# Expert weights in two loads with semaphores of their own, and ring places given back by kind

## The reference

```python
def moe_ffn(h, router_w, router_bias, w_gate, w_up, w_down, s_gate, s_up, s_down):
    top_idx, top_w = route(h, router_w, router_bias)          # 8 of 64 experts for each token
    ...
    yb = lax.map(lambda a: swiglu(a[0], w_gate[a[1]], w_up[a[1]], w_down[a[1]]), (xb, blk_exp))
    ...
    return swiglu(h, s_gate, s_up, s_down) + routed
```

## Time and profile before

| | us |
|---|---|
| median of 3 runs (3470.9 to 3479.81) | 3478.23 |
| the profiled execution | 3474.74 |
| its span | 3472.9 |
| PE busy in the span | 3048.3 (88%) |
| VectorE, ScalarE, POOL busy | 1299.7, 1015.3, 515.6 |

### The profile page before, as it was taken

One profiled execution on the slowest core, in us unless ns is written; L12 is line 12 of the kernel. 1 busy time (PEld: TensorE's weight loads), 2 busy tenths in 40 slices (PEclk: granted clock), 3 DMA queues, 4 the chain that ended last, 5 costly groups with the idle time before them and its releaser, 6 DMA issues. The chain is left out here.

```text
span 3472.9 us, 64620 instructions
## 1 busy us (share of the span) xinstructions
PE 3048.3 (88%) x24428; PEld 1627.9 (47%) x24429; DVE 1299.7 (37%) x2708; ACT 1015.3 (29%) x1799; POOL 515.6 (15%) x534
## 2 busy tenths in 40 slices
PE   6998989979989999999978998899898778867796
PEld 3554668955533333333324546689553223322231
DVE  3434633445433333333354435344443222212234
ACT  2223542222222332333343324422222212222232
POOL 0100005231011111111051100052311000000004
PEclk8998999999999999999989999999899889978898
DMA  9202320032369998998874103200335889887866
GB/s 382 101 10 101 131 88 3 4 132 85 146 230 353 357 354 316 377 358 352 350 285 163 48 7 146 64 3 4 144 158 230 326 338 362 346 338 308 347 262 230
DMA packets 133673, 724.22 MB, mean 209 GB/s; under 512 B 24800, under 2 KB 42720, under 8 KB 96736
## 3 DMA queue, kind: packets, MB, share of 16 engines
q1 hardware_dynamic: 84800, 544.14, 40.4%
q0 software_dynamic: 28224, 102.77, 7.8%
q10 hardware_dynamic: 20448, 74.46, 5.2%
HBM read 619.62 MB, written 101.71 MB: 208 GB/s over the span
## 5 line engine op out<-in xcount | busy, mean ns | idle before, releaser
L2287 PE MATMUL psum<-arena 128*64 x1792 | 830.3, 618 | 184.9 <-DVE arena L2389 184.9
L2289 PE MATMUL psum<-arena 128*64 128x512 f32 x1792 | 830.3, 618 | 0.0
L2287 PEld LDWEIGHTS psum<-arena 128*64 128x64 f32 x1792 | 245.0, 142 | 680.5 <-issue 680.5
L827 PE MATMUL psum<-arena 128*128 128x480 f32 (+3 forms) x1088 | 405.4, 530 | 15.8 <-PEq L164 8.3
L2309 PE MATMUL psum<-arena 128*64 x896 | 408.3, 599 | 12.1 <-DVE arena L2392 8.8
L2311 PE MATMUL psum<-arena 128*64 128x512 f32 x896 | 408.5, 599 | 0.0
L2257 POOL DMA_INDIRECT arena<-h,arena x112 | 141.8, 1266 | 1367.9 <-PE psum L2277 1344.6
L827 PEld LDWEIGHTS psum<-arena 128*128 128x128 f32 x1088 | 209.1, 195 | 190.6 <-issue 178.2
L2356 ACT COPY arena<-arena 128x2048 f32 x114 | 215.9, 1894 | 249.8 <-DMA arena<-in_w_dn 238.8
L2309 PEld LDWEIGHTS psum<-arena 128*64 128x64 f32 x896 | 120.0, 138 | 280.2 <-issue 280.1
L2289 PEld LDWEIGHTS psum<-arena 128*64 128x64 f32 x1792 | 245.0, 142 | 0.0
(11 more groups left out here) (359 smaller groups left out, 4328.7 us busy)
## 6 DMA issues: line engine op xcount, KB each, us to landing
arena<-in_w_gu SPq DMA_DIRECT2D x130, 2048.0 KB
arena<-in_w_dn SPq DMA_DIRECT2D x130, 1024.0 KB
y_slots<-arena ACTq DMA_DIRECT2D x122, 512.0 KB, 10.4
arena<-in_ada SPq DMA_DIRECT2D x24, 2048.0 KB, 7.8
y_slots<-arena SPq DMA_DIRECT2D x4, 4096.0 KB
arena<-in_w_gdn SPq DMA_DIRECT2D x6, 1536.0 KB
arena<-in_w_out SPq DMA_DIRECT2D x2, 4096.0 KB
arena<-in_w_tok SPq DMA_DIRECT2D x4, 1920.0 KB
```

The costliest lines, as they stand in the source:

```text
L827: last = nc.tensor.matmul(bank(n, wide), lhsT[:, k], rhs[:, k], start=(k == 0), stop=(k == DK - 1))
L2287: nc.tensor.matmul(psum[half(0), 2 + r, :], xT[:, r, rows_of(k, 0)], W[:, bass.ds(at + k * 2 * DE, 2 * DE)], start=(k == 0), stop=(k == DK ...
L2289: last = nc.tensor.matmul(psum[half(1), 2 + r, :], xT[:, r, rows_of(k, 1)], late_gu[:, k * 2 * DE:(k + 1) * 2 * DE], start=(k == 0), stop= ...
```

## The change

`w_in` is replaced by two pairs of semaphores, `g_in` for gate/up loads and `d_in` for down loads. The copies of gate/up wait on `g_in` alone, and `copy_dn` gets a wait on `d_in`. A ring place's gate/up part is loaded again when `gu_done` (not `units_done`) has reached the former expert's last unit; the down part still waits on `units_done`. The wait for the load two before is by kind too. The loader still issues gate/up and then down of each expert, in order. The plan holds one row with the late expert's number in place of two rows with semaphore counts; the engines work the counts out of it. The plan values are read one unit at a time, right before `gate`, `copy_dn` and `product`, and no longer at the top of the loop.

```diff
+                        def load_gu(e):
+                            if e >= WRING:
+                                free[e] = sp.value_load(plan[0:1, T_FREE + e - WRING:T_FREE + e - WRING + 1], min_val=1, max_val=NU)
+                                sp.wait_ge(gu_done, free[e])
+                            sp.wait_ge(g_in[e % 2], 16 * (e // 2))
+                            at = e % WRING * WSLOT
+                            sp.dma_start(W[:, at:at + GU], A["w_gu"][...]).then_inc(g_in[e % 2], 16)
+
+                        def load_dn(e):
+                            if e >= WRING:
+                                sp.wait_ge(units_done, free[e])
+                            sp.wait_ge(d_in[e % 2], 16 * (e // 2))
+                            at = e % WRING * WSLOT + GU
+                            sp.dma_start(W[:, at:at + DN], A["w_dn"][...]).then_inc(d_in[e % 2], 16)
+
                         for e in range(3, NE):
-                            r = e % WRING
-                            if e >= WRING:
-                                free = sp.value_load(plan[...], min_val=1, max_val=NU)
-                                sp.wait_ge(units_done, free)
-                            sp.wait_ge(w_in[e % 2], 32 * (e // 2))
-                            sp.dma_start(... A["w_gu"] ...).then_inc(w_in[e % 2], 16)
-                            sp.dma_start(... A["w_dn"] ...).then_inc(w_in[e % 2], 16)
+                            load_gu(e)
+                            load_dn(e)
...
+                def wait_weights(eng, sems, e):
+
+                    eng.wait_ge(sems[0], ((e >> 1) << 4) + 16)
+                    eng.wait_ge(sems[1], ((e + 1) >> 1) << 4)
...
                     @block.vector
                     def _(dve):
-                        def copy_gu(need, at):
-                            for r in range(2):
-                                dve.wait_ge(w_in[r], need[r])
+                        def copy_gu(e, at):
+                            wait_weights(dve, g_in, e)
                             nc.vector.tensor_copy(late_gu[:, 0:GU // 2], W[:, bass.ds(at, GU // 2)]).then_inc(lg_ready, 1)
 
-                        def copy_dn(at):
+                        def copy_dn(e, at):
+                            wait_weights(dve, d_in, e)
                             nc.vector.tensor_copy(late_dn[:, :], W[:, bass.ds(at + GU, DN)]).then_inc(ldn_ready, 1)
...
                         later = later_pairs(dve)
-                        early = [slot(dve, u, 1) for u in range(3)]
-                        need = [weights(dve, u) for u in range(3)]
-                        copy_gu(need[0], early[0])
+                        copy_gu(late_expert(dve, 0), slot(dve, 0, 1))
                         for i in range(NLT):
                             token_weights(ch, i, wk, route_keep)
-                        copy_dn(early[0])
+                        copy_dn(late_expert(dve, 0), slot(dve, 0, 1))
+                        e, at = late_expert(dve, 1), slot(dve, 1, 1)
                         product(0, 0)
-                        copy_gu(need[1], early[1])
+                        copy_gu(e, at)
...
                             with dve.If(later > i):
-                                at = [slot(dve, 2 * i + 1 + r, 1) for r in range(4)]
-                                need = [weights(dve, 2 * i + 3 + r) for r in range(2)]
                                 for r in range(2):
                                     take_hidden(2 * i + r + 1, 1 - r)
-                                    copy_dn(at[r])
+                                    copy_dn(late_expert(dve, 2 * i + r + 1), slot(dve, 2 * i + r + 1, 1))
+                                    e, at = late_expert(dve, 2 * i + r + 3), slot(dve, 2 * i + r + 3, 1)
                                     product(2 * i + r + 2, r)
-                                    copy_gu(need[r], at[r + 2])
+                                    copy_gu(e, at)
                                     right(2 * i + r + 1, 1 - r, 16 * i + 16 + 16 * r)
```

More of the change, by code:

```diff
@@ L2166, in _ @@
                         second = bf[:, 0:NBC].rearrange("p (u h) -> p u h", h=HALVES)[:, :, HALVES - 1]
[L2167 to L2168 removed]
+                        ch(V.tensor_scalar(bf[:, T_LATE:T_LATE + NUC], second, 3.0, -1.0, ALU.max, ALU.add))
                         ch(V.tensor_scalar(bf[:, 0:NBC], bf[:, 0:NBC], -1.0, None, ALU.add))
@@ L2215, in slot, with late_expert @@
                     return eng.value_load(plan[0:1, bass.ds(HALVES * u + h, 1)], min_val=0, max_val=(WRING - 1) * WSLOT)
-                def weights(eng, u):
-                    return [eng.value_load(plan[0:1, bass.ds(u + at, 1)], min_val=32, max_val=16 * NE) for at in (T_EVEN, T_ODD)]
+                def late_expert(eng, u):
+                    return eng.value_load(plan[0:1, bass.ds(u + T_LATE, 1)], min_val=2, max_val=NE - 1)
+                def wait_weights(eng, sems, e):
+                    eng.wait_ge(sems[0], ((e >> 1) << 4) + 16)
+                    eng.wait_ge(sems[1], ((e + 1) >> 1) << 4)
                 def later_pairs(eng):
@@ L2227, in _ @@
                     def _(sp):
-                        sp.sem_inc(w_in[0], 64)
-                        sp.sem_inc(w_in[1], 32)
-                        for e in range(3, NE):
-                            r = e % WRING
-                            if e >= WRING:
-                                free = sp.value_load(plan[0:1, T_FREE + e - WRING:T_FREE + e - WRING + 1], min_val=1, max_val=NU)
-                                sp.wait_ge(units_done, free)
-                            sp.wait_ge(w_in[e % 2], 32 * (e // 2))
[L2236 to L2239, removed]
+                        for sem in (g_in, d_in):
+                            sp.sem_inc(sem[0], 32)
+                            sp.sem_inc(sem[1], 16)
@@ new lines, in _ @@
+                        free = {}
+                        def load_gu(e):
[4 more added lines that the diff above has]
+                            at = e % WRING * WSLOT
+                            sp.dma_start(W[:, at:at + GU], A["w_gu"][l * (NE + 1) + 1 + e].rearrange("p k n -> p (k n)")).then_inc(g_in[e % 2], 16)
@@ L2240, in _ @@
                         for r in range(2):
-                            sp.wait_ge(w_in[r], 32 * (NE // 2))
+                            sp.wait_ge(g_in[r], 16 * (NE // 2))
+                            sp.wait_ge(d_in[r], 16 * (NE // 2))
                         for r, (rows, source) in enumerate(((ys, y_dram), (xs, xres))):
                             e = NE - WRING + r + 1
-                            free = sp.value_load(plan[0:1, T_FREE + e:T_FREE + e + 1], min_val=1, max_val=NU)
-                            sp.wait_ge(units_done, free)
+                            sp.wait_ge(units_done, sp.value_load(plan[0:1, T_FREE + e:T_FREE + e + 1], min_val=1, max_val=NU))
@@ L2360, in _ @@
                         later = later_pairs(act)
-                        early = [slot(act, u, 1) for u in range(3)]
-                        need = [weights(act, u) for u in range(3)]
-                        copy_gu(need[0], early[0])
+                        copy_gu(late_expert(act, 0), slot(act, 0, 1))
+                        e, at = late_expert(act, 1), slot(act, 1, 1)
                         gate(0, 0)
-                        copy_gu(need[1], early[1])
+                        copy_gu(e, at)
                         take_x(2, 0)
+                        e, at = late_expert(act, 2), slot(act, 2, 1)
                         gate(1, 1)
-                        copy_gu(need[2], early[2])
+                        copy_gu(e, at)
                         send(0, 0, 16)
@@ L2371, in _ @@
                             with act.If(later > i):
-                                at = [slot(act, 2 * i + 3 + r, 1) for r in range(2)]
-                                need = [weights(act, 2 * i + 3 + r) for r in range(2)]
                                 for r in range(2):
                                     take_x(2 * i + r + 3, 1 - r)
+                                    e, at = late_expert(act, 2 * i + r + 3), slot(act, 2 * i + r + 3, 1)
                                     gate(2 * i + r + 2, r)
-                                    copy_gu(need[r], at[r])
+                                    copy_gu(e, at)
                                     send(2 * i + r + 1, 1 - r, 16 * i + 16 + 16 * r)
@@ L2708, in run_all @@
                             ob, W, w0, sz, w_in, c_in, T = mixer(l, nq, ring, nxt)
-                            above = carve(sbuf(ring, "above", [P, 2 * D + plan_at(nq)[3] + n_units(nq) + 2 + (2 * nq + 8) * NE], place=w0 + WRING * WSLOT))
+                            above = carve(sbuf(ring, "above", [P, 2 * D + plan_at(nq)[2] + n_units(nq) + 2 + (2 * nq + 8) * NE], place=w0 + WRING * WSLOT))
                             xT = above(2, D)
                             idx = above(n_units(nq) + 2).bitcast(I32)
-                            plan = above(plan_at(nq)[3])[0:1].bitcast(I32)
```

(1 more changed line is left out.)

21 lines of the change are left out of this document (11 added, 10 removed).

## The result

The changed kernel takes 3345.4 us (median of 4 runs, 3340.7 to 3352.6) against 3478.4 for the kernel before: a ratio of 0.962, 95% interval 0.960 to 0.965. The forecast was 3384, its range 3350 to 3425. The two profiled executions stand 125.4 us apart (spans 3472.9 and 3347.5); the one of after was among the slower of its four runs.

What follows compares the result with a forecast made beforehand. Layer 0's stage was taken as bound by TensorE, layer 1's stretch by a loop of latencies between loader and TensorE. 3474.7 - 80 - 7.5 - 4 - 2.8 = 3380.4 us; as a median 3384, range 3350 to 3425.

Steps and rivals of the forecast that it cites:

- The size of it: Layer 1's stretch, 2700 to 3290 us: falls from 590 us to between 496 and 516, taken as -80 us.
- the lead: Before layer 1's stretch, 2626 to 2700 us: DMA has room for one more gate/up load, 5 us.
- the last stall: Layer 1's stretch: its last TensorE stall ends with the gate/up load instead of the down load, 2.5 us.
- the single turn: Layer 1's stretch: a unit with two new experts, holding 18.7 us of DMA work, goes from 26 to some 19 us.
- the starts: Start of both stages: moved plan reads leave net three fewer on VectorE's chain, -2 us a stage, -4 together.
- rival B: Layer 1's stretch: DMA can't hold a higher rate for long; at 358 GB/s -36 us, median 3433 us; chance 0.13.
- Layer 0, -2.8 forecast: Layer 0's stage: TensorE is full, three stalls of 2.8 us in all go; stage expected within 5 us of 738.
- That sits under TensorE's products: Loop's top on VectorE: eight plan reads hold take_hidden back 5.5 us every second unit, hidden by TensorE's work; costed at nothing.
- best end: Whole kernel: 117 us off layer 1's stretch and 14.3 us of other terms, giving 3347 us.
- A: Layer 1's stretch: only the latency split works, nothing is issued earlier; -73 us, median 3398 us; chance 0.16.
- C: Every unit: VectorE's register work passes the 2.6 us of cover and delays TensorE; median 3510 us; chance 0.05.
- D: Loads land no earlier in effect, and stalls come back in another place; within 0.3% of 3478 us; chance 0.04.

Runs made afterwards that it cites:

- half_down_before_layer1: Kernel before, with the down load of expert 8 and later cut to its first half of columns in layer 1 alone: 3434.5 us.
- reads_only: Kernel before, with only the plan values read unit by unit right before gate, copy_dn and product: 3466.9 us, ratio 0.997.
- split_only: Changed kernel, but both parts of a ring place wait for units_done again; copies still wait for gate/up alone: 3410.2 us, ratio 0.982.
- ahead_and_start: Changed kernel, with gate/up of e+1 issued before down of e, and token_weights run after take_hidden(0) at a stage's start: 3330.0 us, ratio 0.959.
- places_only: Changed kernel, but both gate/up copies also wait for the late expert's down load; places still given back by kind: 3382.4 us, ratio 0.973.

## Why the prediction was right in kind and short in size

**The bound, right.** It named layer 1's stretch, a loop between the loader and TensorE, and both edits as ways out of it. 114.8 of the 125.4 us come from there, the split and the places each act alone, and half_down_before_layer1 shows that the kernel before wasn't bound by bytes.

**The step that failed: "The size of it", -80 us.** With the lead and the last stall, which fall inside the same stretch, it stood at -87.5; -114.8 was measured. The reasoning that DMA would bind the whole stretch was right (1.01). The rate was wrong. I placed it between 496 us, the work at the old ratio of share to bytes, and 516, at the 384 GB/s of the earlier trace rows. That row is of a time when TensorE set the pace: its 0.96 was demand and not a ceiling. The 419 GB/s of the other row, taken with a full queue, was the ceiling, and 198 MB at 419 are 473 us, for 477 measured. I had that number, and used it as the far end. Of the ratio, too, more was to be had: before, a full share was worth 336/0.84 = 400 GB/s, after 417/1.01 = 413. The same slip is in the single turn: its 18.7 us of DMA work are 26 us at 282 GB/s, 7.3 MB, which take 17.6 us at 417, and 17.2 to 17.4 were measured for "some 19".

**The lead, -5 of the -87.5.** Some 2 MB more are moved before the stretch, as worked out (20.2 MB from 2626 to 2700, 22.0 from 2619 to 2691). But the stretch itself holds 53 loads of either kind and some 198 to 199 MB in both kernels: the loader is as far ahead at its end as at its start. So no part of the -114.8 can be put down to the lead.

**Where the shortfall lies.** The sum of 3380.4 for the profiled execution met 3349.3, 31 us less: 27 from the stretch, 8 from layer 0, 3 from between the starts and the stretch and behind it, less 3 that the starts didn't give and 4 from ahead of layer 0's stage.

**The Trainium skill's bound.** By the Trainium skill's rule of some 358 GB/s per core for loads from HBM (DMA: Bandwidth & Descriptors, Where 436 GB/s comes from) the stretch would have taken an estimated 554 us (198 MB at 358 GB/s). The trace decides against it for this case, and with it against rival B: 417 GB/s over 477 us, of which all but the results' stores (34 of 0.52 MB, a tenth) are reads. The prediction quoted the rule without what the same section says of it: the Trainium skill has the 358 there as half of what one HBM stack gives its two cores, and beside it a measured 425 GB/s for a load of 16 MB. One core ran here, and its 417 and 423 GB/s are near that second figure; what two at once would get no run shows.

**Layer 0, -2.8 forecast, -11.0 measured** (736.8 to 725.8, second silu to last), outside the 5 us that the prediction's signs allowed it. The stalls' part was about right: reads_only leaves 2.3. The other 8.7 I had costed at nothing: "That sits under TensorE's products". I looked at what waits for take_hidden itself and not at what stands behind it on VectorE's queue, the down copy, which ended 0.2 us or more too late. After layer 1's stretch, too, where the prediction had nothing, the changed kernel gained 2.3 us (96.0 to 93.7); reads_only gives 0.9 of them (95.1), split_only all.

**The starts, -2 each forecast.** The first product came 4.4 us sooner after the first plan read (8.4 to 4.0), as worked out. The second silu came only 0.8 us sooner in layer 0 (27.3 to 26.5) and 0.6 in layer 1, so the term was more than twice too large: the first period grew from 9.2 to 13.2 us. ahead_and_start shows what held it, the token_weights that stand on VectorE before copy_dn and product(0).

**The range.** Its low end, 3350, came from the worked-out best end of 3347, rounded up; 3347 itself lies 2 us above the measured time. Forecast and low end both lacked layer 0's 8.7 us, and the stretch went almost to the best end.

**Rivals.** A (only the split works): refuted; places_only gains more than split_only. Its own size, -73 in the stretch, was too large too: 50.5. C and D (VectorE's arithmetic, stalls elsewhere): every period in layer 0 after the first is 11.7 us, so in the loop nothing came in TensorE's way, and the stretch's gain leaves nothing of D. The new wait in copy_dn costs TensorE nothing that can be seen. Here it holds VectorE back 0.4 us:

```profile
2968.64 1.23 DVE L2404 COPY arena<-arena 128x2048 f32 x1 [0.41 <-DMA arena<-in_w_dn]
```

## What to carry to other kernels

When two engines wait for each other in turn and neither is full, forecast the stage by whichever becomes full, at the rate that it shows in a short time when its queue really is full; a long stretch in which something else sets the pace is no ceiling. Give each load its own semaphore and each part of a buffer its own release, and check that the order of issue doesn't tie them together again: here issuing the larger load one ahead gave 16 us more. When a wait or a read on an engine's queue is costed at nothing, check not the next instruction alone but each one behind it.

## What the runs showed of the hardware

The share of busy DMA engines isn't a measure of work done. With nearly the same bytes in each stretch (197 to 199 MB) a full share was worth 389/0.99 = 393 GB/s with one load of each kind in flight, 400 before, 413 in the changed kernel and 423/1.01 = 419 with gate/up ahead. The kernels with more loads queued moved more in the same busy time; why wasn't tried. And 423 GB/s were held over 466 us, mostly reads from HBM.
